# A decoder step in fp32 split products: thirds of the columns outside, the three terms inside

## The reference

```python
def rglru_mixer(...):
    u = x @ w_in                     # 1024 x 2048
    ...
    r = jax.nn.sigmoid(block_diag(xc, w_a, b_a).astype(jnp.float32))
    ...
    y = (h.astype(x.dtype) * jax.nn.gelu(gate_branch)) @ w_out
def conv_ffn(x, buf, w_up, conv_w, conv_b, w_down):
    u = x @ w_up                     # 1024 x 6144
    ...
    return (jax.nn.gelu(gate) * val) @ w_down, new_buf   # 3072 x 1024
def shared_kv(x, kv_norm, w_kv):
    kv = rmsnorm(x, kv_norm) @ w_kv  # 1024 x 2048
def diff_attn_layer(...):
    q = (x @ w_q).reshape(...)       # 1024 x 1024
    ...
    return o.reshape(bsz, t_len, D_V) @ w_o
```

## Time and profile before

| | us |
|---|---|
| median of 3 runs | 2613.8 |
| lowest and highest | 2613.32, 2615.16 |
| profiled execution: span from the first to the last instruction | 2612.1 |
| PE busy in it | 2585.3 |
| PE weight loads busy | 2531.8 |
| DVE busy | 1450.9 |
| POOL busy | 773.0 |
| ACT busy | 711.9 |

### The profile page before, as it was taken

The page is one execution under the profiler, slowest core; times in us unless marked ns, Lnnn a source line. Parts: engine busy times, 40 slices in busy tenths (PEclk is TensorE's granted clock), DMA queues, the critical chain, the costliest instruction groups (busy, mean ns, idle before and its releaser), DMA issues.

```text
span 2612.1 us, 40388 instructions
## 1 busy us (share of the span) xinstructions
PE 2585.3 (99%) x16892; PEld 2531.8 (97%) x16892; DVE 1450.9 (56%) x2316; ACT 711.9 (27%) x1186; POOL 773.0 (30%) x431
## 2 busy tenths in 40 slices
PE   8999999999999999999999999999999999999998
PEld 7999999999999999999999999899999999999998
DVE  8877464455444445476656555646544544444457
ACT  5655221111111111124444444522111111111112
POOL 2001233232332323334333333032333323233231
PEclk9999999999999999999999999999999999999999
DMA  3112211111111111134233332311111111111112
GB/s 144 43 44 91 73 49 41 49 42 48 49 41 49 43 47 49 41 122 134 86 101 103 96 98 93 148 41 49 47 43 49 41 49 42 48 49 41 49 49 82
DMA packets 82021, 170.08 MB, mean 65 GB/s; under 512 B 9605, under 2 KB 48005, under 8 KB 81582
## 3 DMA queue, kind: packets, MB, share of 16 engines
q1 hardware_dynamic: 75886, 145.18, 17.3%
q10 hardware_dynamic: 5952, 22.30, 2.3%
HBM read 145.93 MB, written 26.23 MB: 66 GB/s over the span
## 4 chain that ended last, share of the span: by engine, by line
PE 94%; DVE 3%; ACT 1%; issue 1%; DMA 0%; SPq 0%; DVEq 0%; ACTq 0%
PE psum L834 74%; PE psum L1030 3%; PE psum L1034 3%; PE psum L1032 3%; PE psum L1064 2%; PE psum L1088 2%; PE psum L1076 1%; PE psum L1266 1%; DVE line L1868 1%; DVE xn_lo L1885 0%; PE psum L1145 0%; DVE x L2511 0%; PE psum L1118 0%; DMA w_raw<-in_w 0%; PE psum L1162 0%
## 5 line engine op out<-in xcount | busy, mean ns | idle before, releaser
L834 PE MATMUL psum<-xn_hi,w_hi 128*128 128x352 f32 x3024 | 654.5, 324 | 1.5 <-issue 0.8
L834 PE MATMUL psum<-xn_lo,w_hi 128*128 128x352 f32 x3024 | 651.8, 323 | 0.0
L834 PE MATMUL psum<-xn_hi,w_lo 128*128 128x352 f32 x3024 | 651.0, 323 | 0.0
L713 POOL TENSOR_SCALAR w_hi<-w_raw 128x1024 fp32r<-128x1024 f32 x158 | 168.8, 1068 | 1350.5 <-PE psum L834 1259.6
L834 PEld LDWEIGHTS psum<-xn_lo,w_hi 128*128 128x128 f32 x3024 | 519.2, 188 | 0.0
L834 PEld LDWEIGHTS psum<-xn_hi,w_hi 128*128 128x128 f32 x3024 | 514.7, 189 | 3.8 <-issue 3.7
L834 PEld LDWEIGHTS psum<-xn_hi,w_lo 128*128 128x128 f32 x3024 | 513.4, 188 | 0.0
L717 POOL TENSOR_TENSOR w_lo<-w_raw,w_hi 128x1024 fp32r<-128x1024 f32 x158 | 407.8, 2581 | 13.2
L1543 ACT ACTIVATE line<-line,columns 128x1072 f32<-128x1072 f32 x96 | 123.3, 1285 | 1057.0 <-DVE line L1851 1057.0
L1892 DVE TENSOR_TENSOR x<-psum,x 128x1056 f32<-128x1056 f32 x192 | 241.3, 1257 | 246.0 <-PE psum L834 243.1
L1846 DVE TENSOR_TENSOR line<-psum,inverse_rms 128x704 f32<-128x704 f32 x102 | 91.0, 893 | 460.7 <-PE psum L834 460.5
(11 more groups left out here) (282 smaller groups left out, 2966.0 us busy)
## 6 DMA issues: line engine op xcount, KB each, us to landing
w_raw<-in_w SPq DMA_DIRECT2D x200, 512.0 KB, 3.5
k_pages<-in_cache_k SPq DMA_DIRECT2D x128, 64.0 KB, 2.0
v_pages<-in_cache_v SPq DMA_DIRECT2D x128, 64.0 KB, 2.1
scratch_line<-scratch_row ACTq DMA_DIRECT2D x1, 4608.0 KB, 22.3
x<-in_x SPq DMA_DIRECT2D x8, 528.0 KB, 8.7
scratch_x<-x ACTq DMA_DIRECT2D x1, 4224.0 KB, 12.5
out_k<-raw ACTq DMA_DIRECT2D x8, 528.0 KB, 2.7
out_v<-raw ACTq DMA_DIRECT2D x8, 528.0 KB, 2.7
```

The source lines that it names most:

```text
L713: pool.tensor_scalar(WHI[:, s], WRAW[:, s], 1.0, 0.0, ALU.mult, ALU.add).then_inc(w_hi, 1)
L834: last = pe.matmul(PS[:, 3 * (a % 2) + c, 0:CH], w[:, s, k, :], r[:, c * CH:(c + 1) * CH], start=start and first, stop=stop and final)
```

## The change

In `product`, the loop over the thirds becomes the outer one and the loop over the three terms the inner one. The start flag still goes to the first term of the first key tile and the stop flag to the last term of the last one, for each third; the nine matmuls, their operands and their banks are the same, and `last` is the last term of the last third in both.

```diff
             def product(s, k, a, hi, lo, start, stop, whi=WHI, wlo=WLO):
 
-                for w, r, first, final in ((whi, hi, True, False), (wlo, hi, False, False),
-                                           (whi, lo, False, True)):
-                    for c in range(NCH):
+                for c in range(NCH):
+                    for w, r, first, final in ((whi, hi, True, False), (wlo, hi, False, False),
+                                               (whi, lo, False, True)):
                         last = pe.matmul(PS[:, 3 * (a % 2) + c, 0:CH], w[:, s, k, :],
                                          r[:, c * CH:(c + 1) * CH],
                                          start=start and first, stop=stop and final)
```

## The result

The changed kernel takes 2598.9 us, the median of four executions, against 2613.8 us before: a ratio of 0.9942, 95% interval 0.9921 to 0.9963, 14.9 us saved. Faster, as forecast, and inside the range, which goes up to 2607, but less than half of the 31 us that the sum gave. What stands out is the spread. The four executions took 2592.5, 2593.4, 2604.4 and 2605.0 us, so that the median lies midway between two pairs, at a time that none of them took; the kernel before stays within 2613.3 and 2615.2. The profile is of one of the two longer executions (2604.4 us, span 2601.9).

A forecast was written before the change was run, and what follows sets the result against it. The prediction took TensorE's matmul stream, busy 2585.3 of 2612.1 us, as the bound. Gaining 2.60 ns on each of 12384 - 460 matmuls saves 31.0 us: 2613.8 - 31.0 = 2582.8, say 2583 us, range 2576 to 2607.

The forecast's parts named there:

- the sum: All L834 matmuls outside three stretches, (12384 - 460) x 2.60 ns, giving 31.0 us saved.
- The bound and the term: TensorE's matmul stream bounds the kernel; only start-to-start spacing at L834 changes, 2.60 ns gained per matmul.
- The stretches where PE's pace doesn't count: Three stretches where the chain runs over DVE and ACT, holding 460 L834 matmuls; PE's saving there becomes waiting.
- quick rhythm: Faster spacing seen in L1030 and output projection, 158.9 to 159.3 ns per matmul, expected at L834 instead of 161.86.
- quick throughout: All L834 streams at about 159.3 ns per matmul, 2583 us; chance 0.52.
- the rhythm term: At L834, the only term with a size: 161.86 ns falls to 159.3, gaining 2.60 ns per matmul.
- The mixture: Rival: stops redraw the pace or it swaps midway; half each gives 160.3 ns, 19 us gained, 2595 us; chance 0.18.
- a run keeps the one it began with: In L1030 to L1034, the same instructions have a quick (158.9 ns) and a slow (161.6 ns) rhythm, kept throughout a run.
- The slow rhythm's gain: Rival: L834 at 161.2 to 161.6 ns throughout, 8 down to 3 us gained, 2606 to 2611 us; chance 0.12.
- The slower rival: If each third at L834 paid for its bank change, 166.7 ns per matmul, 58 us lost, 2671 us; chance 0.08.
- No difference: Rival: spacing depends on width and clock alone, so L834 stays at 161.86 ns, 2611 to 2614 us; chance 0.10.
- Repeated loads at no cost: Weight loads hide behind matmuls, 189 ns beside 324 ns, so changing tiles at each load instead of repeating costs nothing.

The follow-up runs named there:

- experiment 3: Changed kernel with each third's terms reordered to high.high, high.low, low.high, so the data tile changes at every matmul; 2592.3 us.
- experiment 5: Changed kernel plus two 32-column matmuls, one ahead of each FFN's second up unit, behind the norm's sum; 2586.6 us.
- experiment 12: Changed kernel plus six 96-column matmuls: ahead of each FFN's third and fourth up units and the third tiles of w_out and w_o; 2581.7 us.
- experiment 1: The changed kernel run again unaltered, for the spread of its executions; 2592.2 us.
- experiment 6: Changed kernel plus one matmul ahead of each FFN unit but the first, its width going through 23 values from 16 to 344 columns; 2598.2 us.
- experiment 9: Changed kernel with added matmuls of 23 widths, and the PSUM bank changing at every matmul while the data columns stay for three; 2598.7 us.
- experiment 11: Changed kernel with added matmuls of 23 widths, and the high weights in all three terms, so one tile loads nine times running; 2597.4 us.
- experiment 2: Changed kernel's alternating terms, but third, PSUM bank and columns going on at every matmul as in the kernel before; 2605.3 us.

## Why the prediction was right or wrong

- **The bound and the term: right.** Only the distance between two starts moved. The instructions, loads and clock are unchanged, L834's idle time by 0.1 us, and 7.2 of the profile's 10.2 us are in the two FFN rows.
- **The stretches where PE's pace doesn't count: right.** From DVE's step at 1153.46 us to the norm's sum at 1187.53 was 34.07 us before. After, it is 34.09, from 1148.13 to 1182.22 (the other two stretches, 29.8 and 15.2 us, haven't changed either):

```profile
1148.13 1.26 DVE x L1892
...
1182.22 0.79 PE psum L998 x6
```

- **The size of the quick rhythm: nearly right.** A quick FFN gains 2.95 ns for each matmul (158.91 against 161.86), where 2.60 was taken. The changed kernel itself never had both FFNs quick; in kernels near it the lowest execution of experiment 3 took 2579.7 us, that of experiment 5 2580.5, and the median of experiment 12 is 2581.7, where the forecast for quick throughout was 2583.
- **Wrong: the step that failed is the rhythm term, 2.60 ns gained on all 11924 matmuls, and behind it the 0.52 for quick throughout.** In the profiled execution both FFNs gained 0.73 ns, and in the ten executions of the changed kernel, by the times, the two long streams were never both quick; over the 11924 matmuls the 14.9 us are 1.25 ns each. The 0.52 rested on the quick runs of L1030, three in four, as if each were a chance of the whole. The share is read rightly: of the 58 runs with at least 14 matmuls 43 are quick. But they are no draws. In all 14 profiles of this case 57 of these 58 runs are quick or slow in the same places, whatever the order in `product` and the rhythm of the FFNs; only the first one varies. The stretch of the earlier trace rows (25 steps, 4.04 us) comes back after the change, from the second matmul to the last:

```profile
1282.21 0.32 PE L1032 MATMUL psum<-xn_hi,w_lo 128*128 128x352 f32 x1
...
1286.26 0.32 PE L1034 MATMUL psum<-xn_lo,w_hi 128*128 128x352 f32 x1
```

and in experiment 1:

```profile
1269.99 0.32 PE L1032 MATMUL psum<-xn_hi,w_lo 128*128 128x352 f32 x1
...
1274.04 0.32 PE L1034 MATMUL psum<-xn_lo,w_hi 128*128 128x352 f32 x1
```

4.05 us both times. So the three in four count places in the program, and say nothing on the chance of a stream at L834. There each FFN has one lot, for 5040 and 4824 matmuls.
- **The mixture, 160.3 ns and 2595 us, at 0.18, is what the result is,** made of two streams and not of many short pieces. How near the median of four comes to it is luck: no execution took 2598.9 us. The measured gain is 14.9 us, or 21.7 in experiment 1, according to the draw.
- **Wrong as a rule: "a run keeps the one it began with" as a matter of two rhythms.** It keeps it, but there are three in this order, and a single matmul of another width moves the stream between them (experiment 6).
- **The slow rhythm's gain was put a little low.** 161.2 to 161.6 ns was read from short runs, the latter with three steps that take 0.50 us together; the FFNs show 161.13, so even the worst lot gains 9.2 us of device time (2613.8 to 2604.6).
- **The slower rival is out.** A bank change in the slow rhythm was to cost 20 ns for each third; the steps at 800 us show 0.49 and 0.48 us per third, and experiment 9 changes the bank at every matmul for nothing. What the prediction tied to the bank belonged to the columns, which it didn't name at all.
- **"No difference" is out** for the same reason as the rule beside it. The Trainium skill ("TensorE: Matmul & The Clock Gate", section "Back-to-back issue gap") gives, for isolated matmuls, one gap for a width and no term for the order. Here matmuls of 352 columns, each with its weight load, at a granted clock of 0.998 to 0.999, follow each other at 158.9, 160.0, 161.1 or 161.86 ns by their order and by what ran before.
- **Repeated loads at no cost: right** where it was tried alone (experiment 11). Whether the 0.73 ns between before (161.86) and experiment 2 (161.13) come from them, in an order whose columns change, was not tried and stays open.

Open too: what in the chip makes the rhythms, why a change of columns matters, and what differs between executions. It doesn't look like PE's stop for the norm's sum: in three profiles the pace is the same on both sides of it, and the lot falls before, at about the third tile of w_out and of w_o. That it is a matter of phase is the word of the expectations and not shown. With one profile for each experiment, the split of the unprofiled executions rests on their times, and 2592 us is one FFN at 158.9 and one at 161.1, as profiled, or could be both at 160.0.

## What to carry to other kernels

In a TensorE-bound kernel of split products, let the terms that read the same columns stand together; it was worth 0.3 to 1.3% here (9 to 34 us), by the rhythm that the streams fall into. When executions of such a kernel fall into clusters, compare the long chain rows of two profiles before looking for anything else: a stream may keep one of several paces for hundreds of microseconds. A single odd-sized matmul inside the stream can pick the pace. The width has to be found by a sweep, for which one trace is enough, and the order of the widths should change within it, so that each stands behind several rhythms. And many short runs in a quick rhythm are no chance for a long stream: look first whether a second profile has the quick ones in the same places.

## What was unexpected of the hardware

- A steady stream of matmuls of 352 columns, each with a weight load, has discrete paces, 1.11 ns apart (953.3, 960.0 and 966.7 ns for six), each kept over thousands of matmuls (158.9 and 161.1 ns over 5040, 160.0 over 4824). It can keep its pace over a stop of PE: six of six FFN streams had that of the row before.
- An added matmul of 96 columns in the stream costs 0.115 us, as much as 0.7 of a 352-column one, and the pace behind it follows a pattern over widths that repeats from 48 columns on (158.9, 160.0 or 161.1 ns, four of four places each).
- In this stream, changing the PSUM bank at every matmul costs nothing (the same paces behind the widths from 48 columns on); changing the columns of the data at every matmul takes both lower paces away (161.0 to 161.2 ns behind 94 of 94 added matmuls).
